# Two expert layers: from tiles of 128 slots for one expert to fixed slots of 96 and waves of four 32-column tiles

## The reference, cut to what matters

```python
def _moe(h, w_router, b_router, w_gu, w_down):
    probs = jax.nn.softmax((t @ w_router), axis=-1)
    sel = probs + b_router
    ...                       # best group of four, in it the best two: eidx, gates
    gu = jnp.einsum('td,edf->tef', t, w_gu)                     # 1024 -> 2 x 256
    act = jax.nn.silu(gu[..., :D_EXPERT]) * gu[..., D_EXPERT:]
    act = act * gates.astype(act.dtype)[..., None]
    y = jnp.einsum('tef,efd->td', act, w_down)                  # 256 -> 1024
```

## Time and profile before

| | us |
|---|---|
| median of 3 runs (lowest, highest) | 2418.91 (2414.42, 2424.68) |
| profiled execution | 2408.83 |
| its span | 2407.0 |
| PE busy in the span | 1984.3 (82%) |
| DVE, ACT, POOL busy | 811.7, 385.5, 356.7 |

### The profile page before, as it was taken

One profiled execution on the slowest core, in us unless ns is written; L12 is line 12 of the kernel. 1 busy time (PEld: TensorE's weight loads), 2 busy tenths in 40 slices (PEclk: granted clock), 3 DMA queues, 4 the chain that ended last, 5 costly groups with the idle time before them and its releaser, 6 DMA issues. The chain is left out here.

```text
span 2407.0 us, 33215 instructions
## 1 busy us (share of the span) xinstructions
PE 1984.3 (82%) x13493; PEld 1098.1 (46%) x13493; DVE 811.7 (34%) x1666; ACT 385.5 (16%) x872; POOL 356.7 (15%) x476
## 2 busy tenths in 40 slices
PE   5999999998896799737988898898986769759980
PEld 3443434333343444326655655655754634334430
DVE  0123233233423200053255535535535414320007
ACT  1000100000000111132132232232221100011110
POOL 0010101101022000122030031031021002300004
PEclk9999999999998799956998998998895889869995
DMA  9625344350602699793222113023034480159974
GB/s 334 226 83 204 125 146 167 114 175 34 253 40 81 223 350 348 277 347 104 70 85 77 58 52 112 19 85 97 30 113 142 153 255 35 40 183 343 343 258 166
DMA packets 221242, 381.86 MB, mean 159 GB/s; under 512 B 17165, under 2 KB 88469, under 8 KB 221078
## 3 DMA queue, kind: packets, MB, share of 16 engines
q1 hardware_dynamic: 214002, 354.22, 42.3%
q0 software_dynamic: 7104, 25.69, 2.8%
HBM read 305.25 MB, written 74.63 MB: 158 GB/s over the span
## 5 line engine op out<-in xcount | busy, mean ns | idle before, releaser
L545 PE MATMUL bank<-ring,hT 128*128 128x512 f32 x768 | 345.1, 600 | 3.1 <-PEq L262 2.0
L1272 PE MATMUL bank<-hT,ring 128*128 128x272 f32 x1024 | 309.8, 438 | 1.3 <-PEq L879 1.3
L2213 PE MATMUL bank<-ring,exp_xT 128*128 128x512 f32 x512 | 232.8, 608 | 18.3 <-issue 14.6
L545 PEld LDWEIGHTS bank<-ring,hT 128*128 128x128 f32 x768 | 142.3, 191 | 188.3 <-issue 185.6
L1272 PEld LDWEIGHTS bank<-hT,ring 128*128 128x128 f32 x1024 | 196.4, 207 | 56.0 <-issue 21.2
L2791 PE MATMUL bank<-ring,oT 128*128 128x512 f32 x384 | 175.3, 618 | 13.2 <-DMA oT<-oT_spill 12.6
L2213 PEld LDWEIGHTS bank<-ring,exp_xT 128*128 128x128 f32 x512 | 96.8, 194 | 134.9 <-issue 129.9
L2791 PEld LDWEIGHTS bank<-ring,oT 128*128 128x128 f32 x384 | 75.7, 199 | 108.2 <-issue 95.2
L2232 PE MATMUL bank<-ring,exp_aT 128*128 128x512 f32 x256 | 115.4, 593 | 1.6 <-ACT exp_aT L2267 1.6
L1269 PE MATMUL bank<-ring,hT 128*128 128x512 f32 x256 | 112.9, 602 | 0.0
L2302 DVE TENSOR_TENSOR exp_a<-bank,exp_sg 128x256 f32<-128x256 f32 x32 | 13.6, 425 | 278.1 <-ACT exp_sg L2285 278.1
(11 more groups left out here) (437 smaller groups left out, 2535.1 us busy)
## 6 DMA issues: line engine op xcount, KB each, us to landing
ring<-in_moe_w_gu_dram SPq DMA_DIRECT2D x32, 2048.0 KB, 9.3
ring<-in_w_ada_dram SPq DMA_DIRECT2D x24, 2048.0 KB, 9.5
ring<-in_moe_w_down_dram SPq DMA_DIRECT2D x32, 1024.0 KB, 11.6
ring<-in_ret_w_in_dram SPq DMA_DIRECT2D x8, 2048.0 KB, 13.5
ret_Ss<-in_state_ret_dram SPq DMA_DIRECT2D x32, 512.0 KB, 5.1
out_dram<-ret_Ss SPq DMA_DIRECT2D x32, 512.0 KB, 3.9
expert_outputs<-exp_y SPq DMA_DIRECT2D x32, 512.0 KB, 4.7
ring<-in_dn_w_in_dram SPq DMA_DIRECT2D x8, 2048.0 KB, 9.1
```

What stands on the lines that cost most here:

```text
L545: last = pe.matmul(ps[u % 2][:, :], core.hT[:, k, tok(t)], core.ring[:, w % RING, k, :], start=(k == 0), stop=(k == KD - 1))
L1272: mm = pe.matmul(ps[U % 2][:, 0:HALF], core.ring[:, w % RING, k, c * P:(c + 1) * P], core.hT[:, k, half * HALF:(half + 1) * HALF], start=( ...
L2213: last = pe.matmul(ps[v][:, :], xT[:, v, k, :], wgu[v][:, k, :], start=(k == 0), stop=(k == KD - 1))
```

## The change

Every expert gets 96 slots (`CAP`), which are three tiles of 32 (`G`), whatever its count. 16 x 96 slots are 12 waves of 128 rows (`WAVES`); a wave has four 32-column tiles, of one to two experts, and the matmuls of the four go to different column strips of the array and to different partitions of one bank. Tokens ranked 96 and later in an expert go to tiles of 128 of the old kind behind the waves, in a loop, one at a time, with weights fetched in the iteration (`more`). The twelve waves are written out. The weights are fetched in expert order into four slots of their own (three in new memory, one in the unused end of `oT`), the first four from the start of routing. `ring` stays free, so in layer 0 w_ada blocks 13, 14 and 15 are loaded in routing, and at waves 7 and 9, and PE runs the three modulations ahead of the combine's transposes. The DVE instructions for `experts` move behind those that lead to `source`.

```diff
+G = 32
+SHARE = 3
+CAP = G * SHARE
+WAVES = NE * CAP // P
+MAXO = 2 * NTOK // (CAP + 1)
+MAXT = WAVES + MAXO
+SLOTS = 4
...
# routing, SP
-                    sp.wait_ge(core.ada_done, 13)
-                sp.wait_ge(planned, 1)
-                for v in range(2):
-                    e = plan.expert(sp, v)
-                    plan.up_weights(sp, e, v)
-                    if v == 0:
-                        plan.down_weights(sp, e, v)
+                for e in range(SLOTS):
+                    plan.fetch(sp, 0, e)
+                    plan.fetch(sp, 1, e)
                 if l == 0:
+                    core.load(sp, core.ada_w[13])
                     core.modulations_out(sp, 11, 1, res[:, 0:1])
...
# routing, DVE
-                chain(dve.tensor_scalar(start[:], start[:], float(P), None, ALU.mult))
-                chain(dve.tensor_tensor(dest[:], dest[:], row(start[:], NT), ALU.add))
+                chain(dve.scalar_tensor_tensor(start[:], start[:], float(P), rest, ALU.mult, ALU.add))
+                chain(dve.scalar_tensor_tensor(t16[:], ranks, float(CAP), row(start[:], NT), ALU.is_ge, ALU.mult))
+                chain(dve.tensor_tensor(dest[:], dest[:], t16[:], ALU.add))
...
# experts, SP
+                for i in range(WAVES + 2):
+                    if i >= 2:
+                        for e in range(NE):
+                            if last_wave(e) == i - 2:
+                                plan.fetch(sp, 1, e + SLOTS, s["y_done"])
+                        sp.wait_ge(s["y_kept_act"], i - 1)
+                        sp.wait_ge(s["y_kept_dve"], i - 1)
+                        sp.dma_start(yr[:, i - 2, :], y[:, i % 2, :]).then_inc(s[f"y_out{i % 2}"], 16)
+                    for e in range(NE):
+                        if last_wave(e) == i:
+                            plan.fetch(sp, 0, e + SLOTS, s["gu_done"])
+                    if l == 0 and i in (7, 9):
+                        core.load(sp, core.ada_w[14 + (i == 9)])
...
# experts, PE
+                def up(i):
+                    v, of = i % 2, experts_of(i)
+                    pe.wait_ge(s["xT_kept"], 2 * i + 2)
+                    if i >= 2:
+                        pe.wait_ge(s["a_done"], i - 1)
+                    for e in sorted(set(of)):
+                        pe.wait_ge(*plan.arrival(e, 0))
+                    for k in range(KD):
+                        for j in range(P // G):
+                            last = pe.matmul(ps[v][G * j:G * (j + 1), :], xT[:, v, k, G * j:G * (j + 1)],
+                                             wgu[of[j] % SLOTS][:, k, :], start=(k == 0), stop=(k == KD - 1),
+                                             skip_group_check=True)
+                    last.then_inc(s["gu_done"], 1)
...
+                for i in range(WAVES):
+                    turn(i)
+                    if i >= 2:
+                        down(i - 2)
+                    if i:
+                        turn_a(i - 1)
+                    up(i)
...
# combine_features, PE
+                for n in range(13, 16):
+                    core.modulate(pe, n, ps[n - 9])
                 for t in range(NT):
-                    if t == 3:
-                        core.modulate(pe, 13, ps[4])
...
-                for n in (14, 15):
-                    core.modulate(pe, n, ps[n - 9])
...
# Plan
+    def fetch(self, sp, half, last, done=None):
+
+        while self.fetched[half] <= min(last, NE - 1):
+            e = self.fetched[half]
+            if e >= SLOTS:
+                sp.wait_ge(done, last_wave(e - SLOTS) + 1)
+            to, src = ((self.wgu, self.gu), (self.wdn, self.dn))[half]
+            sp.dma_start(to[e % SLOTS], src[:, e]).then_inc((self.gu_in, self.dn_in)[half][e % SLOTS], 16)
+            self.fetched[half] += 1
+
+def experts_of(i):
+    return [(P // G * i + j) // SHARE for j in range(P // G)]
+
+def last_wave(e):
+    return (SHARE * e + SHARE - 1) // (P // G)
```

More of the change, by code:

```diff
@@ L2136, in _ @@
                         core.keep_modulation(dve, n, ps[n - 10], res[:, n - 11, :], core.BIASES["routing"])
+                chain.mark(dve.tensor_copy(exp_f[:, MAXO:MAXO + 1], end[:, NE - 1:NE]))
+                chain(dve.tensor_tensor(exp_t[:], row(end[:], MAXO), bc(tiles, NE), ALU.is_le))
+                chain(dve.tensor_reduce(exp_f[:, 0:MAXO], exp_t[:], AX.X, ALU.add))
+                chain(dve.tensor_scalar(exp_f[:, 0:MAXO], exp_f[:, 0:MAXO], float(NE - 1), None, ALU.min))
+                dve.tensor_copy(plan.experts[:], exp_f[0:1, :]).then_inc(planned, 1)
                 dve.wait_ge(source_ps, 1)
@@ L2155, in experts, with more @@
         y = st.sb("y", [P, 2, D])
-        names = ("turned", "xT_kept", "gu_done", "silu_done",
-                 "a_done", "aT_turned", "aT_kept", "y_done", "y_kept_act", "y_kept_dve", "y_out0", "y_out1", "stores")
+        names = ("turned", "xT_kept", "gu_done", "silu_done", "a_done", "aT_turned", "aT_kept", "y_done", "y_kept_act",
+                 "y_kept_dve", "y_out0", "y_out1", "more_gu_in", "more_dn_in", "more_turned", "more_xT_kept",
+                 "more_gu_done", "more_silu_done", "more_a_done", "more_aT_turned", "more_aT_kept", "more_y_done",
+                 "more_y_kept_act", "more_y_kept_dve", "more_y_out", "stores")
         s = {n: st.sem(n) for n in names}
+        s["more_x_in"] = st.pool_sem("more_x_in")
         yr = d["y_rows"].rearrange("(s p) n -> p s n", p=P)
[L2161 to L2169, removed]
+        def more(eng):
+            return eng.Fori(0, eng.value_load(plan.experts[0:1, MAXO:MAXO + 1], min_val=0, max_val=MAXO))
         with nc.Block() as block:
@@ L2189, in _ @@
[L2189 to L2195, removed]
-                    sp.sem_inc(s["stores"], 1)
[L2198 to L2222, removed]
@@ L2236, in _ @@
             @block.tensor
             def _(pe):
[L2238 to L2247, removed]
@@ L2311, in _ @@
                 st.clear_used(pool)
[L2312 to L2318 removed]
+                for i in range(2, WAVES):
+                    pool.wait_ge(s["turned"], i - 1)
+                    plan.gather(pool, i, i % 2)
+                pool.wait_ge(s["turned"], WAVES)
+                pool.sem_inc(s["more_turned"], 1)
+                with more(pool) as p:
+                    pool.wait_ge(s["more_turned"], p + 1)
+                    plan.gather(pool, p + WAVES, 0, s["more_x_in"])
 def combine(core, l, plan, x_from, x_to):
@@ L2981, in moe_half @@
     mixer_end(core, l, core.oT, x_from, x_mid, plan, logits)
-    routing(core, l, logits, plan)
-    experts(core, l, plan)
+    with ExitStack() as half:
+        plan.weights(core, half, l)
+        routing(core, l, logits, plan)
+        experts(core, l, plan)
+    core.used = core.used + plan.sems
     if l == 0:
```

245 lines of the change are left out of this document (149 added, 96 removed).

## The result

The changed kernel takes 2384.3 us (median of four runs, 2382.07 to 2385.95) where the kernel before takes 2417.89 (four runs). The ratio is 0.986, with a 95% interval of 0.983 to 0.988: faster by 34 us. The prediction said 2340 and a range of 2312 to 2372, so the kernel is faster, as expected, but has only some 40% of the gain, and the time lies outside the range. The two profiled executions are 2408.83 (before) and 2385.92 us.

The account below looks back on a forecast made before the run. In the expert stages neither TensorE nor DMA had slack; the bound was to move to the transfers. Layer 1's 50, layer 0's 25 and 4 after it make 79 us: 2330 profiled, 2340 as the time given, range 2312 to 2372.

Parts of the forecast that it names:

- No count passes 96, so the loop over the rest runs zero times: Expert stages: 52 to 84 tokens an expert, then 56 to 82, so 16 tiles become 12 waves with no loop pass.
- Rival 4: The overflow loop runs, or something else eats half the gain; chance 2%.
- The matmuls of a wave: TensorE, expert stages: 0.108 us a column tile, `up` 6.9 us, `down` 3.5, a wave 11.7 us like a tile before.
- Rival 1: Four column tiles don't run fully side by side: 3.07x, 14.9 us a wave, 2405 us in all; chance 4%.
- The start of layer 0: Layer 0's expert stage: SyncE's issues stall behind a full queue, first transpose at about 822, 12 us later than before.
- The transfers: DMA, expert stages: 5.24 MB a wave, 14.4 us at 365 GB/s (bounds 353, 386); decide layer 0, 25 us less.
- Layer 1: Its expert stage: first transpose 2136.2, TensorE bound 2286.2, transfers 2282.5, plus 3 us for waits: end 2289, 50 us less.
- After layer 0's stage: Modulations leave the tail and w_ada the queue, so ring loads end earlier: 4 us gained, bounds 0 and 6.
- Rival 2: Weight fetches come too late, slot turns keep 12.02 us per expert, 16.0 a wave: no change, 2420 us; chance 6%.
- Rival 3: Waits keep TensorE at 1.2 GHz: 22.5 us a wave, 170 us slower, 2590 us; chance 5%.

Follow-up runs that it names:

- run 2: Changed kernel with the size above which an expert gets a tile of the rest set to 78 instead of 96: 2478.42 us.
- run 1: Changed kernel with that size set to 1100 instead of 96, which no expert can pass, so the loop's count is zero: 2382.66 us.
- the guarded kernel: Changed kernel with the loop over the rest on five engines inside a branch taken only when the count is not zero: 2327.06 us.
- run 5: The guarded kernel with, in layer 0, two experts' fetches and the second modulation slice moved from routing to the experts' program: 2322.8 us.
- run 6: The guarded kernel with 128 slots for each expert instead of 96, so sixteen waves instead of twelve: 2414.57 us, ratio 1.000 to the kernel before.
- run 7: The guarded kernel with room for the weights of three experts instead of four: 2377.73 us.
- runs 3 and 4: Changed kernel with the loop over the rest behind a branch (the guarded kernel), 2327.06 us, and with that loop left out on all engines, 2338.62 us.
- run 8: Kernel of run 5 with the second modulation slice's load moved behind the sixth wave's fetches: 2322.18 us.

## Why the prediction was wrong

**The step that failed** is "No count passes 96, so the loop over the rest runs zero times". Its first half is right (run 2). The second is not: at a count of zero the body runs once (run 1), 30.0 us in layer 0 and 30.7 in layer 1. Rival 4, with 2%, is what came true. It named the loop, but as a matter of counts; I never asked what the loop does when it is empty, although its place behind all waves, with a fetch, two matmul groups and a store in series, made its price easy to read: the rows of before have every part of it. The kernel before had `Fori(1, last + 1)` with a positive count, so its trace could not show it.

With the loop skipped, the same prediction is a good one. It asked for 79 us off the profiled 2408.83, which is 2330; the guarded kernel's profiled run is 2327.06, and its median is 86 us under that of the kernel before in the same series. Its two stages of experts are 30.9 and 48.0 us shorter than before, where 25 and 50 were forecast. The parts, in the changed kernel:

- *The matmuls of a wave.* Predicted 0.108 us a column tile and 6.9 us for `up`; measured 7.07. The wave was to take TensorE 11.7 us and takes 11.96. Rival 1 (3.07x) is refuted; the four-fold packing of the earlier trace rows carries over.
- *The start of layer 0.* Predicted 822, measured 823.88, of which 3.6 us come from earlier stages (routing starts at 777.17 instead of 773.58). That SyncE's issues stall was the right mechanism, as run 5 shows by taking it away; its last issue ends at 823.34, where I said about 820.
- *The transfers.* The mis-sized term: "I take 365"; measured 408 to 414 GB/s. The bound from the saturated row of 386 was still too low. I divided a rate by a share at partial load, and that gave the lower figure; 350 at 0.98 here and 372 at 1.00 in run 6 show that a share near 1 doesn't mean that the queue gives all it can. So layer 0's waves don't end by the transfers (983.7) but by TensorE and one longer wait: the last `down` ends at 979.9, or 976.3 in the clock of the kernel before. The gain up to there was 32 us instead of 25. The Trainium skill ("DMA: Bandwidth & Descriptors", Where 436 GB/s comes from) says that about 358 GB/s, the share of the memory that a core gets, binds a transfer from memory, and 435 only transfers inside the chip. For this single core the windows disagree with the first figure, by 50 GB/s over 80 us. The Trainium skill has on the same page, under Bandwidth, 425 GB/s for 16 MB with one core at work, and gives 358 for each of two that share the memory; the 408 to 414 of this kernel's one core lie near the 425.
- *Layer 1.* Predicted end of the last `down` 2289, first transpose 2136.2. Measured 2283.1 and 2127.34; the routing began 7.1 us earlier than in the kernel before, so on its clock 2290.2 and 2134.4. The 50 us came: 49. That they agree so well is in part luck: the start came 1.8 us earlier than forecast, and the stretch from there to the end took 3.0 us longer, with waves of 11.96 us. The forecast's transfer bound (2282.5) was also set beside TensorE's without the last `down` of 3.6 us behind it, which layer 0's sum has.
- *After layer 0's stage.* Predicted 4 us. From the combine's first load to L926's matmul it is 66.39 us (1014.19 to 1080.58) against 67.57 (1012.36 to 1079.93): 1.2 us. SyncE issues the ring loads 45.2 us after the combine's first load instead of 44.1, behind the combine's stores, and the matmul follows them after 21.2 us instead of 23.5: the shorter queue gives 2.3, and 1.2 are lost ahead of them, where, as I read it, the modulations delay the transposes. The prediction's own working, 4 us less the 1.7 that reach DVE, gave 2.3; it took 4 all the same.
- *Rival 2* (fetches too late) is off with four slots, and run 7 shows what it would have cost: with three slots the gain over the kernel before falls from 86 to 37 us.
- *Rival 3* (the clock): in layer 0 one window was at 0.91, after a wait of 3.34 us, and cost one `up` of 8.69 instead of 7.07 us. Not a mechanism of weight here.

The sum of the profiled executions, by landmarks on SyncE's queue: before routing +3.6, layer 0's routing and experts -1.7 (-32 for the waves, +30 for the body), from its combine to layer 1's routing -8.9, layer 1's routing and experts -18.2 (-49 and +31), the end +2.2. Together -23.0, against 2385.92 - 2408.83 = -22.9. The -8.9 is not the change's alone: 1.2 of it is accounted for above, and the rest lies in the stretch whose time also moved by 15 us between runs 3 and 4.

## What to carry to other kernels

A loop of this kind that is meant to be empty in the usual case has to be looked up in the profile, or guarded by a branch: here an empty one cost 57 us by the medians and 59 by the stages, about two thirds of what the change had to give, and the guard 1.5 to 1.8 us a layer, if that much. Count the fetches on the page against the number that the algorithm needs before anything else; 34 instead of 32 led to the answer. Here TensorE and the transfers bound the stage within a few per cent of each other, and there fewer tiles paid in full only with the deep prefetch (run 7), and reordering the queue only moved the waits (run 8).

## What was unexpected of the hardware

- At a count of zero the loop's body still ran once on every engine (2382.66 us at a count that can't be anything else, 2327.06 with a branch around it). Whether the chip does this or the way in which `Fori` is put into instructions, no run separates.
- The queue's rate from memory with large transfers was 408 to 414 GB/s at a share of 1.03 to 1.04, while saturated stretches of the kernel before gave 367 and 386.
- Issues of SyncE stall when much is outstanding: 2.65 to 8.58 us for a fetch of 1 MB, where an unhindered issue takes 0.4 us. With a shorter queue (run 5) four small stores took 1.85 us instead of 7.62, and the next stage began 14.7 us earlier, since a block's end waits for the engine.
- The same instructions, from layer 0's combine to the end of layer 1's mixer, took 1078 to 1095 us in different kernels that have the new combine; in one stretch of 140 and 150 us the granted clock was 0.95 against 0.87. A comparison of two kernels a few us apart has to look at the stage, not the total.
